# Kernel study: values and states of the first sweep chunk used in place, rotary keys loaded in blocks of 512, first two query tiles loaded and split inside the sweep

## The reference

```python
# layer 0: h @ w_in_e is cut into
(gq, gk, gv, ga_f, ga_b, gz, cq, ckv, kr, mz)
# A: gated linear attention, 4 heads, one scan forward and one backward
o = q.exp(b) @ state + att @ v          # per chunk and direction
state = exp(b_last) * state + (k * exp(b_last - b)).T @ v
# B: latent attention, 4 heads
q = rms_norm(cq) @ w_uq ; kv = rms_norm(ckv) @ w_ukv
kr = apply_rope(kr, cos, sin)           # one rotary key, shared by the heads
s  = qn @ kn.T + qr @ kr.T ; p = softmax(s) ; o = p @ v
y  = concat(o_A * silu(gz), o_B * silu(mz)) @ w_out_e
```

## Time and profile before

| | |
|---|---|
| median of 3 runs | 3161.47 us (3161.12 to 3161.55) |
| the profiled execution | 3163.21 us, span 3161.4 us |
| TensorE busy | 3020.8 us, 96% of the span |
| VectorE, ScalarE, GpSimd busy | 43%, 37%, 21% |
| mean granted TensorE clock | 0.979 of full speed |

### The profile page before, as it was taken

One profiled execution on the slowest core, in us unless ns is written; L12 is line 12 of the kernel. 1 busy time (PEld: TensorE's weight loads), 2 busy tenths in 40 slices (PEclk: granted clock), 3 DMA queues, 4 the chain that ended last, 5 costly groups with the idle time before them and its releaser, 6 DMA issues.

```text
span 3161.4 us, 47932 instructions
## 1 busy us (share of the span) xinstructions
PE 3020.8 (96%) x17252; PEld 2535.6 (80%) x17252; DVE 1364.8 (43%) x2431; ACT 1172.1 (37%) x2092; POOL 655.8 (21%) x614
## 2 busy tenths in 40 slices
PE   4899999989799999998999999999999999999999
PEld 4668888788588888887887888888888888877887
DVE  5267777745477677764325111122222222222011
ACT  3462244555355555553235111223323332322111
POOL 2112111247222222221320001011121121113221
PEclk8999999989899999999999999999999999999999
DMA  6233355587211121212653211112112122134331
GB/s 227 71 117 103 105 157 162 160 272 205 65 53 54 53 58 57 59 53 76 209 176 117 97 73 46 67 60 80 60 65 75 60 72 67 53 130 156 100 106 53
DMA packets 259401, 318.44 MB, mean 101 GB/s; under 512 B 17043, under 2 KB 187283, under 8 KB 256436
## 3 DMA queue, kind: packets, MB, share of 16 engines
q1 hardware_dynamic: 259286, 316.89, 30.8%
HBM read 214.07 MB, written 102.76 MB: 100 GB/s over the span
## 4 chain that ended last, share of the span: by engine, by line
PE 86%; issue 4%; POOL 3%; DVE 3%; ACT 2%; DMA 2%; SPq 0%; POOLq 0%; DVEq 0%; ACTq 0%
PE PS L349 12%; PE PS L351 11%; PE PS L350 11%; PE PS L2264 4%; PE PS L2265 4%; PE PS L2266 4%; PE PS L2415 4%; PE PS L2416 4%; PE PS L2417 4%; PE PS L1715 4%; PE PS L1735 2%; PE PS L1736 2%; PE PS L1737 2%; PE PS L1704 2%; PE PS L1706 2%
## 5 line engine op out<-in xcount | busy, mean ns | idle before, releaser
L349 PE MATMUL PS<-hTh,whi 128*128 128x512 f32 x1664 | 659.6, 396 | 26.4 <-DVE hTl L302 14.5
L351 PE MATMUL PS<-hTh,wlo 128*128 128x512 f32 x1664 | 650.9, 391 | 0.0
L350 PE MATMUL PS<-hTl,whi 128*128 128x512 f32 x1664 | 650.7, 391 | 0.0
L349 PEld LDWEIGHTS PS<-hTh,whi 128*128 128x128 f32 x1664 | 314.3, 189 | 99.9 <-issue 14.0
L351 PEld LDWEIGHTS PS<-hTh,wlo 128*128 128x128 f32 x1664 | 314.0, 189 | 66.4
L350 PEld LDWEIGHTS PS<-hTl,whi 128*128 128x128 f32 x1664 | 314.6, 189 | 63.5 <-issue 0.2
L341 POOL TENSOR_TENSOR whi<-wraw,zero 128x1024 fp32r<-128x1024 f32 x52 | 99.9, 1921 | 1202.6 <-PE PS L351 951.1
L1808 ACT ACTIVATE pb__168<-PS,nm,rq 128x512 f32<-128x512 f32 x256 | 197.7, 780 | 129.2 <-DVE nm L1872 129.2
L2264 PE MATMUL PS<-ow_h,of_h 128*128 128x512 f32 x576 | 225.0, 391 | 7.5 <-DVE oy L2219 7.5
L2265 PE MATMUL PS<-ow_l,of_h 128*128 128x512 f32 x576 | 224.8, 390 | 0.0
L2266 PE MATMUL PS<-ow_h,of_l 128*128 128x512 f32 x576 | 224.7, 390 | 0.0
(11 more groups left out here) (262 smaller groups left out, 5859.9 us busy)
## 6 DMA issues: line engine op xcount, KB each, us to landing
projT<-pev SPq DMA_DIRECT2D x80, 256.0 KB, 2.6
xt<-x SPq DMA_DIRECT2D x8, 2048.0 KB, 9.5
mw<-wmod SPq DMA_DIRECT2D x64, 256.0 KB, 2.8
oxt<-x SPq DMA_DIRECT2D x32, 512.0 KB, 4.7
sg_v<-vev SPq DMA_DIRECT2D x64, 256.0 KB, 2.4
wraw<-wuz SPq DMA_DIRECT2D x32, 512.0 KB, 5.7
vm<-sg_v SPq DMA_DIRECT2D x16, 1024.0 KB, 5.6
sgT<-mT SPq DMA_DIRECT2D x16, 1024.0 KB, 4.4
```

Source lines behind the costliest of these rows:

```text
L349: pe.matmul(PS[:, bank, :], w[1][:, s, k, :], hTh[:, k, b], start=(k == 0), stop=False)
L350: pe.matmul(PS[:, bank, :], w[1][:, s, k, :], hTl[:, k, b], start=False, stop=False)
L351: mm = pe.matmul(PS[:, bank, :], w[2][:, s, k, :], hTh[:, k, b], start=False, stop=(k == KD - 1))
```

## The change

The two blocks below leave out the renumbering of lines and the removed halves of functions that only moved.

```diff
 # proj_sp, at y = NU-1 (chunk 0 of the backward scan)
-                if n >= 0:
+                if 0 <= n < NT - 1:
                     back_store_s(sp, n)
...
-                    back_store_v(sp, n)
+                    if n < NT - 1:
+                        back_store_v(sp, n)
                 if y == NU - 1:
                     level_store(sp, y - 2)
-                    main_vs(sp, 0)
                     sp.wait_ge(s_pb, 8 + NBLK)
 # proj_act, at y = NU-1, ahead of the last eviction
                     for t in range(2):
                         main_factors(act, t)
+                    main_turned(act, 0)
 # main_pe
+            pe.sem_inc(s_mla[0], 16)
...
+                vals = m_vs[t % 4] if t else vv
...
-                    pe.wait_ge(s_pev, NBLK)
+                    pe.wait_ge(s_pev, NBLK - 1 + t)
+                    pe.wait_ge(s_bs, 2 * NT)
...
+                    back = m_vs[s][:, (GH + h // 2) * DV:(GH + 1 + h // 2) * DV] if t else st[:, (NT - 1) % 2, h // 2, :]
 # rotary keys
-        def rope_keys(sp):
-            for dst, r in ((kr32, 0), (krs, 1)):
-                for half in range(4):
-                    src = O_RKR + ROPE // 2 * ((half + r) % 2)
-                    sp.dma_start(dst[half * 32:half * 32 + 32, :], projT[T_GA, src:src + 32, :]).then_inc(s_krl, 16)
+        def rope_keys(sp, tb):
+            if tb:
+                sp.wait_ge(s_krl, E_krl + 80 * tb)
+            for dst, to, src, n in ((kr32, 0, 0, 64), (kr32, 64, 0, 64), (krs, 0, 32, 32), (krs, 32, 0, 64), (krs, 96, 0, 32)):
+                sp.dma_start(dst[to:to + n, blk(tb)], projT[T_GA, O_RKR + src:O_RKR + src + n, blk(tb)]).then_inc(s_krl, 16)
 # lat_sp
+            if t % 4 == 1 and 0 < t // 4 < NB:
+                rope_keys(sp, t // 4)
 # lat_dve, in tiles 3, 7, 11, 15
-                if tb == 0:
-                    dve.wait_ge(s_krl, E_krl + 128)
+                dve.wait_ge(s_krl, E_krl + 80 * (tb + 1))
 # lat_angle: block 1 uses the scratch of block 0
+            turn, mturned = (turns, mturn) if tb >= 2 else (turns0, mturn0)
 # main_sp
+            pos_load(sp, 1)
             load_z(1)
-            for u in range(2):
-                sp.wait_ge(s_las[u], 16 * NT)
-            pos_load(sp, 1)
-            rope_keys(sp)
+            rope_keys(sp, 0)
             load(3)
             load_z(2)
             load_z(3)
             lat_load(sp, 1)
             sp.dma_start(wv[:, :], ...)
+            for u in range(2):
+                sp.wait_ge(s_las[u], 16 * NT)
```

```diff
 # main_sp, end of tile 14
+                if t == NT - 2:
+                    first_queries(sp)
+        def first_queries(sp):
+            sp.wait_ge(s_pss, NB)
+            for u in range(2):
+                sp.wait_ge(s_qn[u], 32)
+                sp.wait_ge(s_qr[u], 64)
+            for u in range(2):
+                sp.dma_start(qraw[:, u, :, :], q_all[:, :, u * P:(u + 1) * P]...).then_inc(s_qi[u], 16)
 # main_pool, end of tile 15
+                if t == NT - 1:
+                    for u in range(2):
+                        query_split(pool, u, 0, u, False)
 # qraw and qsl lie elsewhere (over sqq and sqk)
-        qraw = at("qraw", M0 + 163 * K, [P, 2, 2, P])
-        qsl = at("qsl", M0 + 165 * K, [P, 2, 3, P], F32R)
+        qraw = at("qraw", M0 + 68 * K, [P, 2, 2, P])
+        qsl = at("qsl", M0 + 76 * K, [P, 2, 3, P], F32R)
 # piece_dve
+            if n == 6:
+                for u in range(2):
+                    dve.wait_ge(s_mst[u], 8 * NT)
 # attn_pool
-            split(0, 0, 0)
-            split(1, 0, 1)
 # attn_sp, after its waits on s_qn and s_qr
-            for u in range(2):
-                query(u, u)
```

More of the change, by code:

```diff
@@ L1240, in lat_angle @@
             lim = float(np.nextafter(np.float32(np.pi), np.float32(0)))
-            ang, turn, mturned = (cosb[:, tb % 2, :], turns, mturn) if tb else (ang0[:, :], turns0, mturn0)
+            ang = cosb[:, tb % 2, :] if tb else ang0[:, :]
+            turn, mturned = (turns, mturn) if tb >= 2 else (turns0, mturn0)
             if k == 0:
@@ L1397, in main_sp, with main_turned @@
                 lat_sp(sp, t)
-        def main_act(act):
[L1400 to L1404, removed]
+                if t == NT - 2:
[6 more added lines that the diff above has]
+            for u in range(2):
+                sp.dma_start(qraw[:, u, :, :], q_all[:, :, u * P:(u + 1) * P].rearrange("w p q -> p w q")).then_inc(s_qi[u], 16)
+        def main_turned(act, t):
+            act.wait_ge(s_mkt, t + 1)
+            if t >= 2:
+                act.wait_ge(s_mc, t - 1)
+            act.activation(m_kT[t % 2][:, :], PS[:, 6, 0:2 * P], ACT.Copy).then_inc(s_mkT, 1)
+        def main_act(act):
             def squares(t):
@@ L1417, in main_act @@
             for t in range(NT + 2):
-                if t < NT:
-                    turned(t)
+                if 0 < t < NT:
+                    main_turned(act, t)
                 if t == 0:
@@ L1529, in contribution @@
                     mm = pe.matmul(PS[r, 7, h // 2 * DV:(h // 2 + 1) * DV], m_kT[t % 2][:, h * DK:(h + 1) * DK],
-                                   m_vs[t % 4][:, h * DV:(h + 1) * DV], start=True, stop=True)
+                                   vals[:, h * DV:(h + 1) * DV], start=True, stop=True)
                 mm.then_inc(s_mc, 1)
@@ L1537, in outputs @@
                     pe.wait_ge(s_ms, 2 * t)
-                else:
+                if t < 2:
                     pe.wait_ge(s_gm, 8)
-                    pe.wait_ge(s_pev, NBLK)
+                    pe.wait_ge(s_pev, NBLK - 1 + t)
+                    pe.wait_ge(s_bs, 2 * NT)
                 if t >= 2:
                     pe.wait_ge(s_mog, t - 1)
+                vals = m_vs[s] if t else vv
                 for h in range(GH):
                     o = PS[:, o_bank(t), h * P:(h + 1) * P]
-                    pe.matmul(o, m_vs[s][:, h * DV:(h + 1) * DV], attT[s][:, h, :], start=True, stop=False)
+                    back = m_vs[s][:, (GH + h // 2) * DV:(GH + 1 + h // 2) * DV] if t else st[:, (NT - 1) % 2, h // 2, :]
+                    pe.matmul(o, vals[:, h * DV:(h + 1) * DV], attT[s][:, h, :], start=True, stop=False)
                     pe.matmul(o, m_st[:, t % 2, h // 2, :], qf[t % 2][:, 0, h, :], start=False, stop=False)
-                    mm = pe.matmul(o, m_vs[s][:, (GH + h // 2) * DV:(GH + 1 + h // 2) * DV], qf[t % 2][:, 1, h, :], start=False, stop=True)
+                    mm = pe.matmul(o, back, qf[t % 2][:, 1, h, :], start=False, stop=True)
                 mm.then_inc(s_mo, 1)
@@ L1944, in attn_dve, with query_split @@
             mod1_end(dve)
+        def query_split(pool, N, I, u, used=True):
+            pool.wait_ge(s_qi[u], I * 16 + 16)
+            if used:
+                pool.wait_ge(s_S, N * 4 + 4)
+            pool.tensor_tensor(qsl[:, u, 0:3:2, :], qraw[:, u, :, :],
+                               zero[:, 0:1].unsqueeze(1).broadcast_to([P, 2, P]), ALU.add).then_inc(s_q, 1)
+            pool.wait_ge(s_q, N * 3 + 7)
+            pool.tensor_tensor(qsl[:, u, 1, :], qraw[:, u, 0, :], qsl[:, u, 0, :].bitcast(F32), ALU.subtract).then_inc(s_q, 1)
+            pool.wait_ge(s_q, N * 3 + 8)
+            pool.tensor_tensor(qsl[ROPE:P, u, 2, :], qraw[ROPE:P, u, 1, :], qsl[ROPE:P, u, 2, :].bitcast(F32), ALU.subtract
+                               ).then_inc(s_q, 1)
+            pool.wait_ge(s_q, N * 3 + 9)
         def attn_pool(pool):
             def split(N, I, u):
-                pool.wait_ge(s_qi[u], I * 16 + 16)
-                pool.wait_ge(s_S, N * 4 + 4)
-                pool.tensor_tensor(qsl[:, u, 0:3:2, :], qraw[:, u, :, :],
-                                   zero[:, 0:1].unsqueeze(1).broadcast_to([P, 2, P]), ALU.add).then_inc(s_q, 1)
-                pool.wait_ge(s_q, N * 3 + 7)
-                pool.tensor_tensor(qsl[:, u, 1, :], qraw[:, u, 0, :], qsl[:, u, 0, :].bitcast(F32), ALU.subtract).then_inc(s_q, 1)
-                pool.wait_ge(s_q, N * 3 + 8)
-                pool.tensor_tensor(qsl[ROPE:P, u, 2, :], qraw[ROPE:P, u, 1, :], qsl[ROPE:P, u, 2, :].bitcast(F32), ALU.subtract
-                                   ).then_inc(s_q, 1)
-                pool.wait_ge(s_q, N * 3 + 9)
+                query_split(pool, N, I, u)
             def diagonal(N, I, u):
@@ L2616, in _ @@
             proj_pool(pool)
+            pool.sem_inc(s_q, 6)
             main_pool(pool)
-            pool.sem_inc(s_q, 6)
             pool.sem_inc(s_dg, 2)
```

## The result

| | before | after | after / before, 95% interval |
|---|---|---|---|
| first comparison, 4 runs each | 3161.51 us (3161.12 to 3162.39) | 3141.70 us (3138.80 to 3144.48) | 0.9942 [0.9929, 0.9954] |
| second comparison, 23 and 6 runs | 3160.94 us (3151.98 to 3164.53) | 3142.41 us (3138.65 to 3148.38) | 0.9948 [0.9933, 0.9962] |

By the medians the change gains 18.5 to 19.8 us; the ratios, which aren't the quotients of the medians, stand for 16.4 to 18.3 us. Over all 47 runs of before and 10 of after, the means are 3160.6 and 3142.6 us, 18.0 apart. A median of 3141.5 had been forecast. The profiled execution took 3143.72 us for a span of 3141.9, which is 19.5 less than before.

The account below looks back on a forecast made before the run. TensorE, with 86% of the chain, was taken to bound the kernel. Terms 4.0 + 3.1 + 1.2 + 10.9 + 1.2 - 0.4 = 20.0 us took the median from 3161.47 to 3141.5 us; 8-in-10 range 3138 to 3150.5.

Parts of the forecast that it names:

- term 1: Between projection and sweep: taking tile 0's values in place lets `wq` load earlier, so tile 1's contribution starts 4.0 us earlier.
- term 2: Turn of tile 3: `m_kq` is loaded earlier, so TensorE's 3.2 us wait for `m_kf` shrinks; 3.1 us gained.
- Term 3: Behind the turn of tile 3: TensorE's clock stays up once the gap goes; 1.2 us, bounds 0 and 1.7.
- Rival (a): Early gains (terms 1 to 3) are not carried through the sweep; 12.7 us gained, 3148.8 us; chance 0.16.
- rival (c): Everything gives its upper bound and the sweep's remaining `m_kf` waits shrink too; 24.1 us gained, 3137.4 us; chance 0.10.
- Term 4: Attention's start: first queries loaded and split inside the sweep, so TensorE waits for `og`, not `qsl`; 10.9 us gained.
- Rival (b): Attention's opening hangs on zeroing and its loads, paying back the earlier start; 7.9 us gained, 3153.6 us; chance 0.06.
- Term 5: Attention's opening: TensorE starts at full clock, two thirds chance of losing it again; 1.2 us, bounds 0 and 2.4.
- What it adds: Costs in the sweep: splits beside VectorE's rotary additions, 0.2 us, and key loads by blocks, 0.2 us.

Follow-up runs that it names:

- late part alone: Kernel before, with only the first two query tiles loaded at tile 14 and split at tile 15: 3149.65 us, ratio 0.9962.
- whole keys: Changed kernel with keys loaded whole again (eight 256 KB loads), still ahead of the wait for the last level's store: 3145.18 us.
- in place only: Kernel before, with only tile 0's values and states taken in place: 3155.05 us, ratio 0.9987.
- keys late: Changed kernel with keys of blocks 1 to 3 asked for two tiles later (tiles 7, 11, 15): 3179.72 us, ratio 1.0051.
- the last two attempts: Both on norm row first: ScalarE's scalings of `wq` moved early, 3141.58 us; turn 1 early, 3138.04 us.
- turn 1 early: On norm row first, tile 1's turn put ahead of tile 0's outputs on TensorE, its `m_kT` copy earlier on ScalarE: 3138.04 us, ratio 0.9923.
- norm row first: Changed kernel with ScalarE copying the last norm row before the last query block, TensorE's wait behind the first score bank: 3140.59 and 3138.94 us.

## Why the prediction was right, and where not

The means over the kernels with and without a part, from the table, against the terms:

| term | predicted | pair of profiled runs | mean over kernels |
|---|---|---|---|
| 1, tile 0 in place | 4.0 | 4.2 | 3.4 |
| 2, turn of tile 3 | 3.1 | 3.3 | 2.8 |
| 3, clock behind it | 1.2 | 1.05 | 0.7 |
| 4, queries | 10.9 | 10.85 | 10.7 |
| 5, clock at the attention | 1.2 | 0.7 | 0.2 |

The pair's column is read at the start of tile 1's contribution and of the turns of tiles 3 and 4, from the last sweep matmul to the first score, and from A to M; its first figure is 3.36 and the 0.8 us by which the stage ahead of the change ran later in that execution. The means: S to C 13.84 to 10.0, less 0.4 for the copy; C to T3 23.86 to 21.03; T3 to T4 9.54 to 8.86; T15 to A 32.70 to 22.0; A to M 17.67 to 17.5 (the late part alone, after twice, whole keys).

**Terms 1 and 2** were right in mechanism and size: `wqh` lost its wait for `wq`, and the wait at tile 3 went. The last eviction's store left 0.55 us earlier in a run that came to it 0.8 us later, which is the 1.35 us worked out; in the pair the latents were no bound, for `sqq` follows `wqh` without a wait. But in seven of the nine executions behind term 1's mean `sqq` waits 0.33 to 1.01 us for them, which makes the mean 3.4 and the choice near the upper bound too high. In term 2 one reason was idle. It put the early `m_kq` down to fewer and shorter key loads and to the moved wait together; the kernel with whole keys shows that the wait alone is enough.

**Term 3** came out in the pair, and the executions bear it out by the length of the wait. Where TensorE waited 3.21 or 2.60 us at tile 3 (before, in place only), T3 to T4 took 9.91 and 9.84 us; where it did not wait, 8.86 or 8.87. With the late part only the wait was 1.08 us, and T3 to T4 took 8.86 as well:

```profile
664.14 0.44 PE L1538 MATMUL PS<-ident,m_kf 128*128 128x128 f32 x2 [1.08 <-POOL m_kf L1506]
```

So the worth of this term hangs on how long the kernel before happened to wait, and that wait varies by 2 us. Of the 1.7 us that the low stretch was priced at, 1.05 came out, and 0.40 went into the wait for `m_kf` at tile 4 that was foreseen (667.35, above). Both early parts were carried through the sweep: from S to A it is 185.15 us with the late part alone and 177.2 to 177.4 with all of it, 7.8 to 8.0 less. Rival (a) is dead.

One gain was overlooked. From T4 to T15 it took 116.72 and 117.28 us in the two kernels without an early part, and 114.8 to 115.7 in those with either or both (keys late and the last two attempts left out). TensorE's waits in it are as long as before (6.4 us in all, now 6.8), so this is not what rival (c) had in mind; the granted clock rose from 0.94 to 0.96. The prediction has no term for these 1.0 to 2.5 us, and why the clock is higher there isn't shown.

**Term 4** is the firmest: 10.90 us with the late part alone, 10.46 with all of it (T15 to A). The start was foretold through the order of waits: with `qsl` gone, `og` is next. Rival (b) is dead, as the first weighted sum came 19.9 us earlier and waited for nothing.

**Term 5 is the one mis-sized,** 1.2 against 0.7 in the pair and 0.2 in the mean. Its prices were right. A to M was 17.95 us before and is 15.5 to 15.6 with the clock up throughout, so the low clock did cost 2.4; and behind the shorter pause it costs 1.7 (17.26 and 17.28), as worked out. What failed is the weighing: one chance in three was given to the clock's staying up behind 1.96 us, which would have saved all 2.4, and in none of five executions with that pause did it. In four it fell 0.7 to 1.4 us after the start, in the fifth (late part alone) it was still low, and A to M took 18.30, more than the 17.50 to 17.95 behind the pauses of 12.7 to 12.8 us. With a pause of 0.69 us or less, in five executions, the clock was up from the start on, or within a microsecond of it (turn 1 early), and A to M took 15.53 to 15.90. So the worth was there, and the change gets at most 0.7 us of it.

**What it adds** was rightly small. The splits took 0.7 us longer than worked out, within the cover of 2.1, and from T15 to the last sweep matmul it is 19.03 us with the late part alone and was 19.09 before, so they cost nothing there. Keys in blocks cost 0.2 to 0.7 us against whole ones by T3 to T15 (124.05 and 124.56 against 123.84), if that is more than spread. On the page "GPSIMD Engine Reference", section "Specifications", in the Trainium skill: the first split took 1.06 us where it had taken 0.61, beside VectorE instructions with two SBUF inputs (a subtraction for `ckl` ran from 790.79 for 1.75 us), which agrees with the contention that the page states. The addition beside the splits (793.18) took 0.92 us where its like took 0.69 before (801.90), and the additions' 1631 ns at worst are no more than before, so the microsecond that the rule might have cost did not come.

**The range and the spread.** The forecast's 3141.5 beside 3141.7 owes something to chance: the median of four runs of a kernel that spreads over 10 us could have fallen 2 us to either side. Over all runs the gain is 18.0 us where 20.0 had been summed, and the means over kernels for the five terms add up to 17.8 where 20.4 had been put; terms 1, 3 and 5 are the ones that were taken most too high. The unforeseen gain behind T4 made up for a part of it.

## What to carry to other kernels

Before a wait is removed, look for the next one behind it by name and time; here that gave the attention's start within half a microsecond. A pause of 1.96 us ahead of dense matmuls cost 1.7 us more in clock, almost as much again as it lasted, so it is worth closing to the end: that gained 3.1 us in the medians of ten runs. Filling it with idle matmuls kept the clock up in the trace, but no gain was seen in the median. And compare stretches of the trace between fixed instructions when whole runs spread more than the term in question.

## What the runs showed of the hardware

- The same kernel, the norm row first, was profiled twice: S at 625.61 and at 628.18, M to E 2319.4 and 2315.6. Stages that nobody touched move by 2.6 and 3.8 us. In the repeated runs of before, which spread over 12.8 us, the shorter ones have the higher mean granted clock (0.977 to 0.983).
- Six matmuls whose result nobody reads made the stretch behind them 1.7 us shorter, for 0.2 us of later start (T15 to A 22.24 against 22.08); 0.3 to 0.6 us of it were left at the end.
- The same pause of 1.96 us ahead of the scores came with two costs: A to M took 17.26 to 17.28 us where the clock had risen ahead of it, and 18.30 where it had not.
- A quarter of the bytes in the loads of `krs` landed in 4.5 to 5.1 us, where the whole keys had taken 8.0 to 11.1 and 9.3 to 11.7 (keys whole, wait moved); the loads of `kr` ahead of them took 5.1 to 5.7 after 5.3 to 7.2.
